# The last FFN's up-projection by seven products of quarters, with the sums' low parts made on VectorE

## The chip, the cores and the metric

One NeuronCore of a Trainium2 chip runs the whole program. The metric is device time in microseconds (us), median over runs. PE is TensorE (matmuls), PEld its weight loads, DVE VectorE, ACT ScalarE, POOL GpSimd, SP the engine that issues the DMAs.

## The reference, cut to what matters

Two layers (width 1024) over 1024 prompt tokens and 8 samples of one token each. Each layer adds a recurrent mixer and then a gated FFN (inner width 2816); a last RMSNorm gives the output.

```python
def swiglu(h, w_up, w_down):
    g, u = jnp.split(h @ w_up, 2, axis=-1)
    return (jax.nn.silu(g) * u) @ w_down
...
        x = x + mix
        x = x + swiglu(rmsnorm(x, norm_ffn[layer]), ffn_w_up[layer], ffn_w_down[layer])
    return (rmsnorm(x, norm_final), ...
```

## The kernel before, in words

Tokens lie on the free axis, in two parts: A (columns 0 to 511) and B (512 prompt columns and the 8 samples, 520 in all). Every dense product is a float32 product made of three single-pass ones: an operand is split into a high part (`wh`, `xh`, `hidh`: the value rounded to fp32r, written by ACT) and a low part (`wl`, `xl`, `hidl`: value minus high part), and PE adds high x high, high x low and low x high in PSUM. Weights come in blocks of 128 x 1024 into a ring of four slots; ACT makes `wh` of each (L1162), POOL `wl` (L1428). A block of an up-projection is eight 128-row slices of the input width for 128 output rows.

The inner width is 22 tiles `f`, taken in 11 pairs `g`. For a pair PE does four `up` units (gate and up of two tiles, `dense`, L807) and then eight `down` units of the pair before (L862). In part B a unit's 520 columns are two matmuls of 260 in two PSUM banks; four banks (0 to 3) go round over the units, and a unit may start only when DVE has emptied its bank. DVE multiplies gate and up by the norm's factor `rsB` and with each other (L1598, L1835), ACT does SiLU, POOL a second multiplication (L1534); DVE makes `hidl` (L1841) and adds each `down` unit to `xB` (L1822). The last pair of B is done in two halves of 260 columns (`down_half`, L878; L2101 adds them), so that the final norm of the first half overlaps the second.

`order()` writes one list of items for the whole program, and every engine walks it in that order; so an instruction of an engine stands behind all items ahead of it there. `("up",1,A,g,q)` is a unit, `("xs",n,m)` the squares of norm `n`, `("mx",1,B,h)` the split of head tile `h` of the mixer's result, `("nrm",n)` and `("nrv",n)` norm `n`'s column sum and root. The program ends with FFN 1 of A, output projection 1 of B (`out`, 8 units) and FFN 1 of B.

Of the kernel before, what the change touches and what calls it, by code (L numbers as in the profile page):

```python
# [9 lines left out]
ALU = mybir.AluOpType  # L10
# [33 lines left out]
def _columns():  # L44
    at = 0
    for name, n in (("gmix0", 8), ("gmix1", 8), ("gffn0", 8), ("gffn1", 8), ("gfin", 8), ("blr", 2),
# [12 lines left out]
         (A, None), (B, "gffn1"), (B, None))  # L59
# [3 lines left out]
N_FFN = {(0, A): 2, (0, B): 4, (1, A): 6, (1, B): 8}  # L63


def order():
# [4 lines left out]
    def ffn(L, X, n_next, at, halves=False):  # L71
        for g in range(NG):
            for q in range(4):
# [21 lines left out]
        if halves:  # L95

            for c in range(2):
                for m in range(KT):
                    add(("dh", c, X, m))
                    if m:  # L100
                        add(("xe", c, m - 1))
                    if c and m == 2:
                        add(("ne", 0))
                    if c and m == 4:
                        add(("nr",))
                    if c and m == 6:
                        add(("nx", 4))
                add(("xe", c, KT - 1))
            add(("nx", 5))
            add(("nx", 6))  # L110
            add(("nx", 7))
            add(("fe", 0))
            add(("ne", 1))
            add(("fe", 1))
            return
        for m in range(KT):
            add(("down", L, X, NG - 1, m))
            if m:
                add(("xs", n_next, m - 1))
        add(("xs", n_next, KT - 1))  # L120
# [120 lines left out]
    def rows(X):  # L241
# [19 lines left out]
class Plan:  # L261


    def __init__(self):
# [3 lines left out]
        used = [None] * 4  # L268
# [7 lines left out]
        for x in it:  # L276
# [3 lines left out]
            if k not in ("sm", "in", "z", "out", "up", "down", "dh", "rg", "s1"):  # L280
# [11 lines left out]
            cur += nb  # L292
# [8 lines left out]
            self.free[u] = before  # L301
            e = "A" if k == "rg" else "D"
# [15 lines left out]
            elif k == "dh":  # L318
                g = NG - 1
                if x[1:] == (0, B, 0):  # L320
                    new = [NB + B_FFN + 4 + g * 6, NB + B_FFN + 5 + g * 6]
                    down["dh"] = [len(self.blocks), len(self.blocks) + 1]
                else:
                    for n in down["dh"]:
                        src_end[n] = u
# [2023 lines left out]
```

## Time and profile before

| | us |
|---|---|
| median of 3 runs | 2490.19 (2488.18 to 2491.6) |
| profiled execution, its own time | 2490.38 |
| its span | 2488.6 |
| PE busy | 2434.4 (98%) |
| DVE / ACT / POOL busy | 1007.4 (40%) / 870.9 (35%) / 1098.4 (44%) |

The span goes from the first to the last instruction of the trace; the execution's own time is 1.8 us longer. Matmuls are pipelined, so a row gives 0.28 us for one of 260 columns whose successor starts earlier; the pace is read from starts. PE's granted clock is in the top tenth in all 40 slices of the page.

### The profile page before, as it was taken

The page shows a single profiled execution, that of the slowest core. Times are in us where ns is not written, and L with a number is a line of the kernel's source. Part 1 is how long each engine was busy: PE and PEld are TensorE (multiplying, and loading weights), DVE is VectorE, ACT ScalarE, POOL GpSimd, SP SyncE. Part 2 cuts the span into 40 slices and gives each one's busy share as a digit, 9 for nine tenths or more (in the row PEclk, how much of TensorE's full clock was granted, in tenths as well). Part 3 has the DMA queues.
Part 4 walks back from the last instruction along what each step waited for, and adds up shares of the span by engine and source line. Part 5 has one row for each costly group of instructions (what it writes and reads, how often), then busy time and mean ns, then how long its engine had stood idle before and what let it go on. Part 6 is the DMA issues. An engine that isn't in the chain of part 4 may idle for free.

```text
span 2488.6 us, 37223 instructions
## 1 busy us (share of the span) xinstructions
PE 2434.4 (98%) x15510; PEld 2194.1 (88%) x15510; DVE 1007.4 (40%) x1712; ACT 870.9 (35%) x1155; POOL 1098.4 (44%) x605
## 2 busy tenths in 40 slices
PE   8999999899999999999999899999999999999998
PEld 6889997688887977999999889988887889999998
DVE  4513255334444435543333443344434443222224
ACT  5431135234223355443333244343432334222223
POOL 2722145555465344544354450043545544544453
PEclk9999999999999999999999999999999999999999
DMA  8863373321324477422222274432232334222222
GB/s 302 307 222 136 136 255 118 105 84 63 123 69 134 161 258 265 152 73 94 85 78 94 77 256 179 168 95 78 81 116 96 119 118 163 93 87 93 94 85 86
DMA packets 102246, 335.88 MB, mean 135 GB/s; under 512 B 12288, under 2 KB 16192, under 8 KB 102080
## 3 DMA queue, kind: packets, MB, share of 16 engines
q1 hardware_dynamic: 102080, 333.52, 39.3%
q8 instruction: 123, 2.02, 0.3%
q14 instruction: 43, 0.35, 0.0%
HBM read 255.20 MB, written 76.16 MB: 133 GB/s over the span
## 4 chain that ended last, share of the span: by engine, by line
PE 88%; DVE 5%; POOL 2%; issue 2%; ACT 1%; DVEq 1%; POOLq 1%; DMA 1%; SPq 0%; ACTq 0%
PE ps L807 63%; PE ps L862 18%; POOL wl L1428 1%; DMA wr<-in_wblk 1%; PE ps L902 1%; PE ps L958 1%; PE ps L956 1%; PE ps L831 0%; DVE mixl L1812 0%; ACT wh L1162 0%; DVE sq L1598 0%; POOLq L1445 0%; PE ps L1019 0%; PE ps L1016 0%; PE ps L962 0%
## 5 line engine op out<-in xcount | busy, mean ns | idle before, releaser
L1428 POOL TENSOR_TENSOR wl<-wr,wh 128x1024 fp32r<-128x1024 f32 (+1 forms) x328 | 791.5, 2427 | 553.2 <-ACT wh L1162 552.9
L807 PE MATMUL ps<-xh,wh 128*128 128x260 f32 (+2 forms) x3296 | 881.8, 322 | 6.6 <-issue 2.6
L807 PE MATMUL ps<-xl,wh 128*128 128x260 f32 (+2 forms) x3296 | 868.8, 318 | 0.0
L807 PE MATMUL ps<-xh,wl 128*128 128x260 f32 (+1 forms) x3280 | 866.8, 319 | 0.0
L807 PEld LDWEIGHTS ps<-xh,wh 128*128 128x128 f32 (+1 forms) x3296 | 543.6, 188 | 60.9 <-issue 17.9
L807 PEld LDWEIGHTS ps<-xl,wh 128*128 128x128 f32 (+1 forms) x3296 | 543.0, 187 | 44.8 <-issue 2.4
L807 PEld LDWEIGHTS ps<-xh,wl 128*128 128x128 f32 x3280 | 541.5, 188 | 44.9
L1162 ACT ACTIVATE wh<-wr 128x1024 fp32r<-128x1024 f32 (+1 forms) x332 | 342.6, 1044 | 291.3 <-DMA wr<-in_wblk 283.8
L862 PE MATMUL ps<-hidh,wh 128*128 128x260 f32 (+1 forms) x1024 | 280.8, 328 | 20.3 <-POOL wl L1428 10.3
L862 PE MATMUL ps<-hidl,wh 128*128 128x260 f32 (+1 forms) x1024 | 277.5, 324 | 0.0
L862 PE MATMUL ps<-hidh,wl 128*128 128x260 f32 (+1 forms) x1024 | 276.6, 324 | 0.0
L1287 ACT ACTIVATE sq<-sq 128x512 f32<-128x512 f32 (+1 forms) x88 | 55.9, 635 | 610.0 <-DVE sq L1598 609.9
L862 PEld LDWEIGHTS ps<-hidh,wh 128*128 128x128 f32 x1024 | 172.2, 190 | 42.5 <-issue 14.0
L1822 DVE TENSOR_TENSOR xB<-ps,xB 128x520 f32<-128x520 f32 x184 | 128.6, 699 | 170.4 <-PE ps L862 106.5
L1534 POOL TENSOR_TENSOR sq<-sq,rsB 128x520 f32<-128x520 f32 x44 | 60.1, 1365 | 293.2 <-ACT sq L1287 293.2
L862 PEld LDWEIGHTS ps<-hidh,wl 128*128 128x128 f32 x1024 | 172.1, 190 | 16.0
L862 PEld LDWEIGHTS ps<-hidl,wh 128*128 128x128 f32 x1024 | 172.6, 191 | 14.4
L1534 POOL TENSOR_TENSOR sq<-sq,rsA 128x512 f32<-128x512 f32 x44 | 57.4, 1305 | 277.7 <-ACT sq L1287 277.5
L1835 DVE TENSOR_TENSOR hf<-ps,sq 128x512 f32<-128x512 f32 (+1 forms) x88 | 61.0, 693 | 292.6 <-PE ps L807 278.8
L1822 DVE TENSOR_TENSOR xA<-ps,xA 128x512 f32<-128x512 f32 x192 | 129.2, 687 | 106.9 <-PE ps L862 78.5
L1292 ACT ACTIVATE hidh<-hf 128x512 fp32r<-128x512 f32 (+1 forms) x88 | 55.9, 635 | 209.7 <-DVE hf L1835 209.7
L1598 DVE TENSOR_TENSOR sq<-ps,rsB 128x520 f32<-128x520 f32 x44 | 30.8, 699 | 186.3 <-PE ps L807 180.2
(373 smaller groups left out, 2314.1 us busy)
## 6 DMA issues: line engine op xcount, KB each, us to landing
wr<-in_wblk SPq DMA_DIRECT2D x328, 512.0 KB, 3.6
split<-wh SPq DMA_DIRECT2D x64, 512.0 KB, 5.3
split<-wl SPq DMA_DIRECT2D x64, 512.0 KB, 6.3
wh<-split SPq DMA_DIRECT2D x64, 512.0 KB, 3.2
wl<-split SPq DMA_DIRECT2D x64, 512.0 KB, 4.2
xr<-in_xT SPq DMA_DIRECT2D x8, 260.0 KB, 6.3
xB<-in_xT SPq DMA_DIRECT2D x8, 260.0 KB, 6.3
out_yT<-xB SPq DMA_DIRECT2D x8, 260.0 KB, 2.2
```

Of the source, the lines that this page charges most:

```text
L807: mm = pe.matmul(ps[0:cols, b + c, 0:n], wt[:, w], xt[:, e:e + n], start=first, stop=end)
L862: mm = pe.matmul(ps[:, b + c, 0:n], wt[:, w], xt[:, t + lo:t + lo + n], start=first, stop=end)
L902: mm = pe.matmul(ps[:, b + c, 0:n], lhsT, src[0:p, lo:lo + n], start=True, stop=True)
L956: pe.matmul(ob, QZ[X][:, h * C:(h + 1) * C], S[:, (h // 2) * P:(h // 2 + 1) * P], start=True, stop=False)
L1162: act.activation(hi, raw, ACT.Copy).then_inc(s_hi, 1)
L1287: act.activation(t, t, ACT.Silu).then_inc(s_si, 1)
L1292: act.activation(hidh[:, t], hf[:, t], ACT.Copy).then_inc(s_hh, 1)
L1428: pool.tensor_tensor(lo, raw, hi.bitcast(F32), ALU.subtract).then_inc(s_lo, 1)
L1534: pool.tensor_tensor(t, t, rs[X][:], ALU.mult).then_inc(s_sr, 1)
L1598: mm = v.tensor_tensor(cut(dst, X), src, cut(rs[X][:], X), ALU.mult)
L1822: v.tensor_tensor(t, bank(pl.bank[u], X), t, ALU.add).then_inc(s_evd, 1)
L1835: v.tensor_tensor(cut(hf[:, t:t + W[X]], X), bank(pl.bank[u], X), cut(sq[q // 2][:, 0:W[X]], X), ALU.mult).then_inc(s_evd, 1)
```

## The change

For each tile `f` of the last FFN (layer 1, part B) the weights are seen as a 2 x 2 matrix of quarters: rows gate and up, columns the two halves of the input width, each quarter four 128 x 128 blocks (512 columns of SBUF). The input is 2 x 2 too: halves of the width, halves of the 520 columns (Q = 260). The four results (gate and up of two column halves) come from seven products of quarters or of sums of quarters instead of eight. The sums of the input are made once, those of the weights (`s1` to `s4`) for each `f`.

- Loads: two blocks of `f` into `wqr[f % 2]` (`weight_set`); the `down` blocks of the last FFN have slots of their own.
- `set_sums` ("wS"): four DVE subtractions or additions of 128 x 512. `set_hi` ("wH"): four ACT copies (1024, 512, 1024, 1024 columns). Low parts: `set_lo`, POOL, three quarters from HBM as 128 x 512 instructions; `sums_lo` ("wL"), DVE, the four sums as two of 128 x 1024. `down_lo` is four of 128 x 512 on POOL for a pair.
- `product` ("sp", f, i): 4 k-steps x 3 matmuls of 260 columns. Products 2 and 4 use banks 4 and 5, the others go round with banks 0 to 3. `products_sum` and `first_product` add the products up: one ACT copy of 260, seven DVE additions of 260, then SiLU of the gate on ACT (520) and a product of gate and up on DVE (520, two inputs in SBUF). POOL's multiplication is gone.
- The input must be normalised before it is split: `scaled` (8 DVE instructions of 520), `quarter_sum` (4 of 1040), `quarter_hi` (7 ACT copies of 1040), `quarter_lo` (7 DVE of 1040).
- For that, `out` of B with its squares now stands after the `up` units of A's pair 9, ahead of the `down` units of A's pair 8; the `mx` items are earlier; the work on the input goes between A's remaining units. A's final norm and output go into B's FFN (f = 4 to 20).

```diff
-    ffn(1, A, 7, merge(rows(B), scan(...), ...
-                       {(8, 4): [("ue", 0), ("dma", "smp1out")], (9, 0): [("ue", 1)], (9, 2): mix(1, B)[0:2],
-                        (9, 3): mix(1, B)[2:4], (9, 4): mix(1, B)[4:6], (10, 0): mix(1, B)[6:8]}))
-    out(1, B, 8, {2: [("nrm", 7), ("nrv", 7)], ...
-    ffn(1, B, 9, {}, halves=True)
+    ffn(1, A, None, merge(rows(B), scan(...), ...
+                          {(8, 2): mix(1, B)[4:6], (8, 4): [("ue", 0), ("dma", "smp1out")], (9, 0): [("ue", 1)] + mix(1, B)[6:8],
+                           (9, 1): mix(1, B)[0:2], (9, 2): mix(1, B)[2:4], (9, "end"): outs,
+                           (9, "down", 2): [("nrm", LAST)], (9, "down", 3): [("nrv", LAST)],
+                           (9, "down", 5): [("wS", 0)], (9, "down", 6): [("xn", 0)], (9, "down", 7): [("xn", 1), ("xn", 2)],
...
+    for f in range(2, NF):
...
+        elif f % 2:
+            places = ((f - 2, "down", 6), (f - 1, 0), (f - 1, 1), (f - 1, 2), (f - 1, 4))
+        else:
+            places = ((f - 1, 3), (f - 1, 4), (f - 1, 5), (f - 1, "down", 1), (f - 1, "down", 4))
+        for n, p in enumerate(places):
+            put(p[0], p[1:], ("wH", f, n - 1) if n else ("wS", f))
+        put(places[4][0], places[4][1:], ("wL", f, 2))
+        last = (2, 1) if f == 2 else (3, 0) if f == 3 else (f - 1, 5) if f % 2 else (f - 1, "down", 6)
+        put(last[0], last[1:], ("wL", f, 3))
...
+                for k in range(KT // 2):
+                    w, e = slice(PIECE[i] * 512 + k * P, PIECE[i] * 512 + (k + 1) * P), slice(k * Q, (k + 1) * Q)
+                    for wt, xt, first, end in ((wqh[f % 2], xqh[i], k == 0, False), (wqh[f % 2], xql[i], False, False),
+                                               (wql[f % 2], xqh[i], False, k == KT // 2 - 1)):
+                        mm = pe.matmul(ps[:, b, 0:Q], wt[:, w], xt[:, e], start=first, stop=end)
...
+            def set_lo(f, j):
+                if j > 1:
+                    return
+                pool.wait_ge(s_qhi, 4 * f + j + 1)
+                pool.wait_ge(s_wsum, f + 1)
+                for n in range(*PAIRS[j]):
+                    e = slice(512 * n, 512 * n + 512)
+                    last = pool.tensor_tensor(wql[f % 2][:, e], wqr[f % 2][:, e], wqh[f % 2][:, e].bitcast(F32), ALU.subtract)
...
+            def set_sums(f):
+                a11, a12, a21, a22, s2, s1, s4, s3 = (wqr[f % 2][:, 512 * n:512 * n + 512] for n in range(8))
+                v.drain()
+                v.wait_ge(s_wq[f % 2], 32 * (f // 2 + 1))
+                v.tensor_tensor(s1, a21, a22, ALU.add)
+                v.tensor_tensor(s3, a11, a21, ALU.subtract)
+                v.drain()
+                v.tensor_tensor(s2, s1, a11, ALU.subtract)
+                v.drain()
+                v.tensor_tensor(s4, a12, s2, ALU.subtract).then_inc(s_wsum, 1)
...
+            def products_sum(it, f, i):
...
+                if i == 1:
+                    v.tensor_tensor(gsum[:, 0:Q], part(1), p1[:], ALU.add).then_inc(s_evd, 1)
+                elif i == 3:
+                    v.tensor_tensor(usum[:], part(3), p1[:], ALU.add).then_inc(s_evd, 1)
+                elif i == 4:
+                    v.tensor_tensor(p1[:], part(4), usum[:], ALU.add)
+                elif i == 5:
+                    v.tensor_tensor(gsum[:, Q:2 * Q], part(5), p1[:], ALU.add).then_inc(s_evd, 1)
+                else:
+                    v.tensor_tensor(usum[:], part(6), usum[:], ALU.add).then_inc(s_evd, 1)
+                    v.drain()
+                    v.tensor_tensor(hf[:, t + Q:t + 2 * Q], part(4), usum[:], ALU.add).then_inc(s_evd, 1)
+                    v.tensor_tensor(hf[:, t:t + Q], usum[:], part(2), ALU.subtract).then_inc(s_evd, 1)
+                    v.drain()
+                    v.wait_ge(s_gsi, f + 1)
+                    v.tensor_tensor(hf[:, t:t + 2 * Q], hf[:, t:t + 2 * Q], gsum[:], ALU.mult).then_inc(s_hm, 1)
```

DVE in a pair of the last FFN, before: four units of gate and up (`L1598`, `L1835`) and eight `down` units into `xB`.

```order
L1598 TENSOR_TENSOR sq_65<-ps,rsB 128x520 [waits unit]
L1835 TENSOR_TENSOR hf<-ps,sq_65 128x520 [waits unit,sr]
L1598 TENSOR_TENSOR sq_66<-ps,rsB 128x520 [waits unit]
L1841 TENSOR_TENSOR hidl<-hf,hidh 128x520 [waits hh]
L1835 TENSOR_TENSOR hf<-ps,sq_66 128x520 [waits unit,sr]
L1822 TENSOR_TENSOR xB<-ps,xB 128x520 [waits unit] x2
L1841 TENSOR_TENSOR hidl<-hf,hidh 128x520 [waits hh]
L1822 TENSOR_TENSOR xB<-ps,xB 128x520 [waits unit] x6
```

The same place in the change, an odd `f` from its product 3 to the first `down` units (`wqr` holds the weights' quarters and sums, `p`, `usum` and `gsum` the sums of products).

```order
L1932 TENSOR_TENSOR usum<-ps,p_116 128x260 [waits unit]
L1903 TENSOR_TENSOR wqr_97<-wqr_97 128x512 [waits wq0]
L1904 TENSOR_TENSOR wqr_97<-wqr_97 128x512
L1906 TENSOR_TENSOR wqr_97<-wqr_97 128x512
L1908 TENSOR_TENSOR wqr_97<-wqr_97 128x512
L1934 TENSOR_TENSOR p_116<-ps,usum 128x260 [waits unit]
L1936 TENSOR_TENSOR gsum<-ps,p_116 128x260 [waits unit]
L1938 TENSOR_TENSOR usum<-ps,usum 128x260 [waits unit]
L1940 TENSOR_TENSOR hf<-ps,usum 128x260
L1941 TENSOR_TENSOR hf<-usum,ps 128x260
L1944 TENSOR_TENSOR hf<-hf,gsum 128x520 [waits gsi]
L2153 TENSOR_TENSOR xB<-ps,xB 128x520 [waits unit] x2
```

Ahead of the first `down` sum there are now four sums of weights, five of products and the product of gate and up. DVE's next rows there, to the end of the `down` units:

```order
L2174 TENSOR_TENSOR hidl<-hf,hidh 128x520 [waits hh]
L2153 TENSOR_TENSOR xB<-ps,xB 128x520 [waits unit] x3
L1916 TENSOR_TENSOR wql_99<-wqr_97,wqh_101 128x1024 [waits qhi]
L2153 TENSOR_TENSOR xB<-ps,xB 128x520 [waits unit] x2
L1916 TENSOR_TENSOR wql_99<-wqr_97,wqh_101 128x1024 [waits qhi]
L1903 TENSOR_TENSOR wqr_98<-wqr_98 128x512 [waits wq1]
L1904 TENSOR_TENSOR wqr_98<-wqr_98 128x512
L1906 TENSOR_TENSOR wqr_98<-wqr_98 128x512
L1908 TENSOR_TENSOR wqr_98<-wqr_98 128x512
L2153 TENSOR_TENSOR xB<-ps,xB 128x520 [waits unit]
```

Two low parts and the sums of the next set now stand between `down` sums. DVE at the end of A's last FFN, before (the 16 `down` units of pairs 9 and 10; two of the 16 are in the row ahead):

```order
L1835 TENSOR_TENSOR hf<-ps,sq_66 128x512 [waits unit,sr]
L1822 TENSOR_TENSOR xA<-ps,xA 128x512 [waits unit] x2
L1841 TENSOR_TENSOR hidl<-hf,hidh 128x512 [waits hh]
L1822 TENSOR_TENSOR xA<-ps,xA 128x512 [waits unit] x14
```

and the first rows of that place in the change (`xq` and `xqr` are quarters of B's input, `xqh` and `xql` their parts):

```order
L2153 TENSOR_TENSOR xA<-ps,xA 128x512 [waits unit] x2
L1896 TENSOR_TENSOR xql_83<-xq,xqh_90 128x1040 [waits xh]
L2174 TENSOR_TENSOR hidl<-hf,hidh 128x512 [waits hh]
L2153 TENSOR_TENSOR xA<-ps,xA 128x512 [waits unit] x2
L1896 TENSOR_TENSOR xql_84<-xq,xqh_91 128x1040 [waits xh]
L2153 TENSOR_TENSOR xA<-ps,xA 128x512 [waits unit] x2
L1896 TENSOR_TENSOR xql_85<-xqr_80,xqh_92 128x1040 [waits xh]
L2153 TENSOR_TENSOR xA<-ps,xA 128x512 [waits unit]
L1916 TENSOR_TENSOR wql_99<-wqr_97,wqh_101 128x1024 [waits qhi]
L2153 TENSOR_TENSOR xA<-ps,xA 128x512 [waits unit]
L1896 TENSOR_TENSOR xql_86<-xqr_81,xqh_93 128x1040 [waits xh]
```

Seven `xql`, two `wql` and four sums of weights now stand between the same 16 sums.

## Rows read from the trace of the kernel before

**Rows 1.** The page: busy time of each engine, and granted clock in 40 slices.
```profile
PE 2434.4 (98%) x15510; PEld 2194.1 (88%) x15510; DVE 1007.4 (40%) x1712; ACT 870.9 (35%) x1155; POOL 1098.4 (44%) x605
...
PEclk9999999999999999999999999999999999999999
```
**Rows 2.** Windows: busy time by engine; output projection of B, then two pairs.
```profile
2046.00:2092.40 46.40, 46.40 (x382) 45.88 (x381) 18.17 (x22) 15.43 (x22) 16.15 (x12) 1.00 0.58 205
...
2300.00:2334.60 34.60, 34.60 (x290) 34.60 (x290) 9.61 (x14) 8.66 (x11) 16.80 (x9) 1.00 0.28 92
2334.60:2369.20 34.60, 34.60 (x290) 34.60 (x290) 9.61 (x14) 8.58 (x11) 16.80 (x9) 1.00 0.28 92
```
**Rows 3.** The chain that ended last: start us, us; one pair of the last FFN.
```profile
2221.00 23.03 PE ps L807 x192
2244.04 11.60 PE ps L862 x96
2255.63 23.07 PE ps L807 x192
```
**Rows 4.** Timeline of PE in `down_half`: start us, us; weights change at each.
```profile
2472.82 0.28 PE L878 MATMUL ps<-hidh,wh 128*128 128x260 f32 x1
2472.94 0.28 PE L878 MATMUL ps<-hidl,wh 128*128 128x260 f32 x1
```
**Rows 5.** Groups, 2060 to 2440 and 2440 to 2489: busy us, mean ns, idle before.
```profile
L1822 DVE TENSOR_TENSOR xB<-ps,xB 128x520 f32<-128x520 f32 x78 | 54.6, 700 | 66.0 <-PE ps L862 46.1 <-PE ps L807 18.6
...
L1534 POOL TENSOR_TENSOR sq<-sq,rsB 128x520 f32<-128x520 f32 x21 | 27.5, 1310 | 147.8 <-ACT sq L1287 147.8
...
L2101 DVE TENSOR_TENSOR xB<-ps,xB 128x260 f32<-128x260 f32 x16 | 6.8, 428 | 6.5 <-PE ps L878 6.4
```
**Rows 6.** `hidl`: count, shortest/median/longest ns, first and last start.
```profile
L1841 DVE TENSOR_TENSOR hidl<-hf,hidh x20: 687/690/1623, 2112.0 to 2420.7; 128x520 fp32r<-128x520 f32 x20
```
**Rows 7.** Timeline of DVE and POOL near 2118 and 1976 us.
```profile
2117.29 2.40 POOL L1428 TENSOR_TENSOR wl<-wr,wh 128x1024 fp32r<-128x1024 f32 x1 [0.79 <-ACT wh L1162]
...
2118.62 1.62 DVE L1841 TENSOR_TENSOR hidl<-hf,hidh 128x520 fp32r<-128x520 f32 x1 [0.70 <-ACT hidh L1292]
...
1974.02 7.12 POOL L1428 TENSOR_TENSOR wl<-wr,wh 128x1024 fp32r<-128x1024 f32 x3
...
1976.58 2.25 DVE L2088 TENSOR_TENSOR oc<-oc,oq 128x32 f32<-128x32 f32 x1
1978.90 2.28 DVE L2090 TENSOR_TENSOR vm<-oc,gt 128x32 f32<-128x32 f32 x1
```
**Rows 8.** Timeline of DVE and POOL where B's mixer result is split.
```profile
1985.73 5.22 POOL L1428 TENSOR_TENSOR wl<-wr,wh 128x1024 fp32r<-128x1024 f32 x2
...
1986.00 5.50 DVE L1812 SCALAR_TENSOR_TENSOR mixl<-vm,par,mixh 128x520 fp32r<-128x520 f32 x2 [2.23 <-ACT mixh L1280]
...
2009.89 8.07 POOL L1428 TENSOR_TENSOR wl<-wr,wh 128x1024 fp32r<-128x1024 f32 x3
...
2011.02 4.66 DVE L1814 TENSOR_TENSOR mixl<-vm,mixh 128x520 fp32r<-128x520 f32 x2 [3.12 <-ACT mixh L1282]
```
**Rows 9.** Who waited for whom, 1660 to 2489 us: total, times, longest.
```profile
PE ps L892 <- POOL rsB L1451: 1.3, 1, 1.3
PE ps L862 <- POOL wl L1428: 1.2, 2, 0.6
PE ps L862 <- DVE xA L1822: 1.2, 1, 1.2
```
**Rows 10.** Groups of ACT: the copies behind `wh` and one of 260 columns.
```profile
L1162 ACT ACTIVATE wh<-wr 128x1024 fp32r<-128x1024 f32 x328 | 341.2, 1052 | 284.4 <-DMA wr<-in_wblk 283.8
...
L1201 ACT ACTIVATE rsB<-ps,par 128x260 f32<-128x260 f32 x1 | 0.5, 478 | 1.1 <-PE ps L886 1.1
```
**Rows 11.** Timeline of PE's `down` unit in A, three matmuls.
```profile
1880.16 0.39 PE L862 MATMUL ps<-hidh,wl 128*128 128x512 f32 x1
1880.39 0.40 PE L862 MATMUL ps<-hidh,wh 128*128 128x512 f32 x1
```

More of the change, by code:

```diff
@@ L84, in ffn @@
                     add(("nrm", N_FFN[L, X]))
+            for s in at.get((g, "end"), ()):
+                add(s)
             if g:
@@ L87, in ffn @@
                     add(("down", L, X, g - 1, m))
+                    for s in at.get((g, "down", m), ()):
+                        add(s)
                     if m == 1:
@@ new lines, in order @@
+    for g in range(NG):
+        first, second = ((3, 0), (3, 2)) if g == 0 else ((2 * g + 2, 5), (2 * g + 3, 0)) if g < NG - 1 else ((NF - 1, 3), (NF - 1, 5))
+        put(first[0], first[1:], ("wD", g, 0))
+        put(second[0], second[1:], ("wD", g, 1))
+    for m in range(KT):
+        put(4 + m + m // 2, (2,), ("xs", 8, m))
+    put(16, (0,), ("nrm", 8), ("nrv", 8))
+    for m in range(0, KT, 2):
+        put(17 + m // 2, (1,), ("fin", m))
+        put(17 + m // 2, (4,), ("fin", m + 1))
+        put(17 + m // 2, (6,), ("fo", m))
@@ L279, in __init__ @@
                 self.rs_end[x[1]] = rs_cur[NORMS[x[1]][0]]
-            if k not in ("sm", "in", "z", "out", "up", "down", "dh", "rg", "s1"):
+            if k not in ("sm", "in", "z", "out", "up", "down", "dh", "rg", "s1", "sp"):
                 continue
@@ L301, in __init__ @@
             self.free[u] = before
+            if k == "sp":
+                i = x[2]
+                if i == 0:
+                    count["A"] += 1
+                    self.ev[u] = ("A", count["A"])
+                else:
+                    self.ev[u] = ("D", count["D"] + (0, 1, 6, 2, 5, 3, 4)[i])
+                    if i == 6:
+                        count["D"] += 6
+                self.evac[x] = self.ev[u][1]
+                continue
             e = "A" if k == "rg" else "D"
@@ L317, in __init__ @@
                 new = [NB * x[1] + B_FFN + (0 if g == 0 else 4 + (g - 1) * 6) + q]
[L318 to L325, printed above, removed]
-                    self.blk[u] = down["dh"]
+            elif k == "dh" or k == "down" and x[1:3] == (1, B):
+                continue
             elif k == "down":
@@ L997, in gla_sample_end @@
                     pe.wait_ge(s_q2, 1)
-                    pe.matmul(ps[:, 5, 64:128], ones, osq[:], start=True, stop=True).then_inc(s_qm2, 1)
+                    pe.matmul(ps[:, 5, 64:128], ones, osq[:], start=True, stop=True).then_inc(s_qm, 1)
             def mlstm_columns(X):
@@ L1101, in _ @@
                     pass
+                elif k == "sp":
+                    product(u, *v)
                 elif k == "dh":
@@ L1604, in x_split @@
                 X, g = NORMS[n]
-                if not g:
+                if not g or n == LAST:
                     return
```

350 lines of the change are left out of this document (285 added, 65 removed), and 5 rows, old and new, of the table outs.

## The prediction

> **What bounds the kernel now.** I read the page's busy times first: PE 2434.4 us of 2488.6, and its granted clock is in the top tenth in every slice, the 2.4 GHz level [rows 1]. Then the windows (their columns: stretch, length, then busy time and count of PE, PEld, DVE, ACT and POOL, clock, DMA share, GB/s): in the output projection of B and in the pairs of the last FFN PE is busy for the whole length, with DVE at 9.61 us and POOL at 16.8 us of 34.6 [rows 2]. A pair takes 34.63 us from start to start, 23.04 for 192 `up` matmuls and 11.6 for 96 `down` matmuls [rows 3], so 0.120 us for a matmul of 260 columns. Nearly all PE idle time behind 1660 us is in three short waits [rows 9]. So a matmul saved here is saved in the end, if nobody else becomes late; and the DVE has 25 us of room in a pair.
>
> **What is removed.** A product has 12 matmuls, a tile `f` 84 where it had 96. Over 22 tiles that is 264 matmuls. In `up` before, two matmuls in a row had the same weights; in a product each has others. `down_half` already works like that, and its starts are 0.12 apart [rows 4]. So the price is 264 x 0.120 = **31.7 us** off. A unit (12 matmuls, also a `down` unit of B) is 1.445 us, a pair of the change 22 units, 31.8 us. "TensorE: Matmul & The Clock Gate" of the Trainium skill, Back-to-back issue gap, gives N/2.4 + 2.5 ns, 111 ns at 260; the rows are 9 ns above it. By the page the saving would be 29.3 us, 2.4 less; the measurement decides.
>
> **What the other engines get.** DVE durations: 0.70 for 520 columns out of PSUM, 0.428 for 260 [rows 5], so 1.05 ns a column; with two inputs in SBUF 0.69 for 520 [rows 6], and by the same slope 0.68 for 512, 1.22 for 1024, 1.24 for 1040 (estimates). A drain costs 0.07: L2090 starts that much after L2088 ends [rows 7]. A pair on DVE: 14 sums of products 6.0, 8 sums of weights 5.5, 4 low parts 4.9, 2 products of gate and up and 2 `hidl` 2.8, 8 `down` sums 5.6, 24 drains 1.7: 26.4 us of 31.8, where it had 9.6. ACT: two sets of copies, 3584 columns each, at 1.05 for 1024, and two `down` blocks, 9.6; two 260-column copies at 0.48 and four of 520 at 0.67, by the slope between these two rows [rows 10], 3.6; 13 us. POOL: L1534 does 520 columns in 1.31 [rows 5], so 10 pieces of 512 are 13 us, less than the 16.8 before. ACT and POOL stay far from the bound. Loads are as many bytes as before.
>
> **Where DVE is late, in a pair.** An odd `f`, t = 0 at the start of its first product. Product 3 is over at 4 x 1.445 = 5.8; its last matmul ends 0.16 behind the next start (a row is 0.28 long, the starts 0.12 apart [rows 4]), so DVE starts at 6.0. Behind it stand `usum` 0.43, the four weight sums with three drains 2.93, five sums of products with four drains 2.43, the product of gate and up with its drain 0.76, and the first `down` sum 0.70: 7.25, to 13.2. PE wants that bank for the third `down` unit at 9 x 1.445 = 13.0. With the way back PE waits 0.3. Further on, a `wL` (1.29) between two `down` sums (0.70 each) makes 2.9 where PE gives 2.89, and `wL`, four sums and `down` 7 make 5.8 from the end of `down` 6, with 5.78 till product 3 wants the bank: some 0.1 each. So 0.5 in a pair if nothing collides.
>
> POOL collides. `hidl` started at 2118.62 while a POOL instruction ran from 2117.29 to 2119.69, and took 1.62 in place of 0.69; it ended 0.55 behind POOL's end. Two instructions of 32 columns took 2.25 and 2.28 under three POOL instructions of 2.4 [rows 7]. Sums out of PSUM are not touched: their mean over 78 is 0.700 [rows 5]. So a DVE instruction with two SBUF inputs waits for the running POOL instruction, and gets in before the next: L1812 twice took 5.50 beside two POOL instructions in 5.22, L1814 twice 4.66 beside three in 8.07, where undisturbed three take 7.12 [rows 7, 8]. "SBUF — State Buffer" of the Trainium skill, SBUF: two separate sides, says that the shared port pair is an exclusive lock for the whole instruction and that the loser fully blocks. By that rule the trace agrees, and it speaks against a change that gives DVE 16 such instructions in a pair in place of two.
>
> The collision on the path is the product of gate and up. Its set's sums end at 9.3; POOL's three low parts then run back to back, 9.4 to 10.7, 12.0 and 13.3. DVE wants the pair at 11.8, waits till 12.0 if all is in time, and 1.3 us more if it comes 0.2 later. So the pair's stall is between 0.5 and 2.2 (0.3 + 1.3 + the small ones with one more collision); I take 1.1, nearer the lower end, since the plan meets the gap. It recurs at the nine odd `f` from 3 to 19 (the last has no set to make): 9 x 1.1 = **10 us**, bounds 4.5 and 20. In an even `f` DVE has 6.9 us of work in 10.1, and its banks are wanted four units later: nothing.
>
> **The passage from A to B.** Behind A's pair 10 stand the 16 `down` units of A, 6 matmuls of 0.23 [rows 11], 22.0 us. DVE has 16 sums of 512, about 0.61 each when queued, 9.8; seven `xl` 9.1; two `wL` 2.6; four sums 2.9; `hidl` 0.7: 25.1. POOL still makes two low parts of 2.4 and three of 1.3, 8.7; half of that as waiting of DVE gives 29.5. Four banks of A leave DVE 3.2 of lag, so PE waits 29.5 - 22.0 - 3.2 = **4.3** (0 if nothing collides, 9 if all does). Ahead of that DVE is less full. `out` of B now starts right behind A's `up` units of pair 9, about 1988, where the last sample head ends at 1981.18 [rows 7]; DVE then has 7.1 us of sums, `hidl` and six or so `mixl`, more with the collisions that stood there [rows 8], so PE waits 2 or 3 at its first k-steps and loses the 1.2 and 0.6 that it lost there [rows 9]: **+1**, bounds -1 and +4. B's loads and its norm lie under 55 us of A. A's final norm adds eight products of 512 and a reciprocal of 512 to DVE in f = 16 to 20, up to 0.7 in an odd `f`: **+1**, bounds 0 and 3. The end (`down_half`, last norm) is the same code, with its weights long there: 0.
>
> **Sum.** 2490.4 (the profiled execution's own time, 0.2 above the median) - 31.7 + 10 + 4.3 + 1 + 1 = **2475**. With the lower bounds 2490.4 - 31.7 + 4.5 - 1 = 2462, with all upper ones 2490.4 - 31.7 + 20 + 9 + 4 + 3 = 2495.
>
> **Rivals.**
> - *DVE keeps up.* The handovers are shorter than I take them, POOL's pieces fall beside DVE's: time 2463, range 2458 to 2467. For it: my stall without collisions is only 0.5 in a pair, and 5 us of DVE's time is free. Against it: two rows of the chain have no margin. Chance 0.2.
> - *DVE becomes the bound, slower.* Every second one of the 16 instructions with two SBUF inputs meets a whole POOL piece of 1.31: 10.5 us, so DVE needs 36.9 for a pair where PE needed 34.6 before: (36.9 - 31.8) x 10 + 6 of passages - 31.7 = +25, 2515. It decides from a stall of (31.7 - 6) / 10 = 2.6 in a pair, that is DVE waiting 8 us in a pair. For it: POOL is busy for 13 of 31.8 us, and all sixteen are queued among it. Against it: `set_lo` waits for the sums, so it never meets those four, and most of `wL` come later. Chance 0.13, with what lies just above 2495.
> - *Given back in full, within 0.2%.* The pair's stall is 2 us (the product of gate and up meets the third piece each time, and `wL` one) and the passage costs 9: 2490.4 - 31.7 + 18 + 9 + 2 = 2488. Chance 0.15.
> - *The passage fails.* ACT waits in order for a ring block ahead of `wH` or `xh`, and product 0 of f = 0 starts some 8 us late; the pairs are as I think: 2483. It is in the forecast's upper range.
>
> **How the numbers follow.** Mine 0.52 (2468 to 2484). Within 0.2% (5 us, about what a measurement of this kernel can tell from no change) 0.15, slower 0.13, faster 0.72. The range leaves out half of the slower case and the lowest end: 2461 to 2490.
>
> **What the changed kernel's profile would show.** Product matmuls 0.120 apart; a pair of 32.9 us with PE idle in front of the third `down` unit, released by DVE's `xB` sum; DVE busy 26 to 29 us in a pair; the product of gate and up 0.9 long or more where undisturbed it is 0.69, sums out of PSUM at 0.43; PE gaps of some 4 us in all in A's last 16 `down` units. A pair above 34.4 would show the second rival, one of 31.9 the first. I would be wrong at the root if product matmuls took longer than 0.120, through weights that change each time beside three writing engines.

## The result, and the profile after

The changed kernel takes 2496.64 us, median of 12 runs (2491.53 to 2500.49), beside 2490.26 of before on the same chip (12 runs, 2486.53 to 2491.79): a ratio of 1.0025, interval 1.0016 to 1.0034. It is slower by a little more than what can be told from no change. The profiled execution took 2495.07 us, 4.7 above the one of before. The page of the changed kernel, span and busy times:

```profile
span 2493.1 us, 37403 instructions
...
PE 2412.8 (97%) x15246; PEld 2165.7 (87%) x15246; DVE 1200.8 (48%) x1987; ACT 910.4 (37%) x1222; POOL 1071.3 (43%) x627
```

The 264 matmuls are gone, and PE is busy 21.6 us less [rows 1]; the rest of the span is waiting. The chain, one ordinary pair (start us, us; L1023 is the product, L1054 a `down` unit):

```profile
2187.88 15.89 PE ps L1023 x132
...
2204.69 1.37 DVE wqr L1903
2206.06 1.70 DVEq L1905
...
2207.84 0.69 DVE wqr L1906
...
2210.41 0.43 DVE usum L1938
...
2211.79 0.73 DVE hf L1944
2212.51 0.62 DVE xB L2153
2213.18 9.00 PE ps L1054 x72
2222.18 7.35 PE ps L1023 x60
```

132 matmuls in 15.89 us are 0.120 each, as forecast, so the saving was made. "TensorE: Matmul & The Clock Gate" of the Trainium skill, Back-to-back issue gap, has a formula for a single matmul by which the gap would be 0.111 (an estimate); the row is above it, as before. The pair takes 34.30 us where it took 34.63 [rows 3]. The windows of four pairs, two ordinary ones and the two in which A's final norm runs (columns as in [rows 2]):

```profile
2187.88:2222.18 34.30, 32.34 (x267) 31.86 (x266) 25.76 (x39) 12.48 (x17) 15.11 (x11) 1.00 0.27 93
2256.14:2291.31 35.17, 32.64 (x266) 31.94 (x266) 26.97 (x39) 13.00 (x18) 16.39 (x12) 1.00 0.26 91
2360.00:2398.60 38.60, 35.59 (x267) 34.56 (x266) 28.50 (x41) 17.02 (x21) 14.63 (x10) 0.91 0.29 96
2398.60:2435.26 36.66, 33.89 (x266) 33.09 (x266) 29.95 (x43) 11.96 (x16) 15.01 (x10) 0.95 0.34 116
```

DVE is not the bound: it has 8 us to spare in a pair in which PE waits. What PE waits for, 2097 to 2470 us (total, times, longest), and in the passage, 2046 to 2097:

```profile
PE ps L1054 <- DVE usum L1938: 12.9, 9, 2.5
PE ps L1054 <- DVE xB L2153: 5.3, 10, 0.7
...
PE ps L1054 <- DVE xA L2153: 4.5, 2, 2.3
PE ps L1054 <- POOL wl L1663: 1.4, 1, 1.4
```

The larger wait is once a pair, and not where the forecast has it: PE stands before the second `down` unit, whose bank is that of product 6, and which `usum` (L1938) reads. Some 0.6 us more go at the third, whose bank the first `down` sum empties. The timelines of DVE, POOL and PE there:

```profile
2204.69 1.37 DVE L1903 TENSOR_TENSOR wqr<-wqr 128x512 f32<-128x512 f32 x1 [0.46 <-issue]
2205.99 1.77 DVE L1904 TENSOR_TENSOR wqr<-wqr 128x512 f32<-128x512 f32 x1
2207.84 0.69 DVE L1906 TENSOR_TENSOR wqr<-wqr 128x512 f32<-128x512 f32 x1
```
```profile
2202.97 2.55 POOL L1691 TENSOR_TENSOR dwl<-dwr,dwh 128x512 fp32r<-128x512 f32 x2 [0.82 <-ACT dwh L1405]
2205.68 1.54 POOL L1674 TENSOR_TENSOR rsA<-rsA,sq 128x512 f32<-128x512 f32 x1 [0.16 <-issue]
2209.44 4.22 POOL L1684 TENSOR_TENSOR wql<-wqr,wqh 128x512 fp32r<-128x512 f32 x3 [2.23 <-DVE wqr L1908]
```
```profile
2210.90 0.51 PE L1054 MATMUL ps<-hidh,dwh 128*128 128x260 f32 x2 [1.38 <-DVE usum L1938]
```

A weight sum takes 0.69 undisturbed. The first started under the second half of `down_lo` (L1691) and ended 0.54 behind POOL's end (2205.52), the second under the addition of A's squares (L1674) and ended 0.54 behind that one's (2207.22): together 1.8 us late. PE pays for them with 1.38 us at the second `down` unit and 0.58 at the third. The product of gate and up (L1944), which the forecast lets collide with `set_lo` (L1684), took 0.73 here. Groups of DVE over nine pairs, 2120 to 2430 us:

```profile
L1916 DVE TENSOR_TENSOR wql<-wqr,wqh 128x1024 fp32r<-128x1024 f32 x36 | 46.9, 1302 | 3.2
L1904 DVE TENSOR_TENSOR wqr<-wqr 128x512 f32<-128x512 f32 x18 | 21.0, 1168 | 0.0
L1903 DVE TENSOR_TENSOR wqr<-wqr 128x512 f32<-128x512 f32 x18 | 17.3, 963 | 3.1 <-issue 1.8
L1944 DVE TENSOR_TENSOR hf<-hf,gsum 128x520 f32<-128x520 f32 x18 | 15.9, 886 | 1.6
L1906 DVE TENSOR_TENSOR wqr<-wqr 128x512 f32<-128x512 f32 x18 | 14.3, 795 | 1.3
```

**The balance.** The first product starts at 2096.48, the first tile's matmul of before at 2092.99: 3.5 later. From there to the first `down_half` unit it is 371.3 us, before 370.2; the 2808 matmuls of that stretch at their pace (11.56 us for 96) would take 338.1, so some 33 us are lost inside. The starts of the even tiles' first products (2153.45, 2187.72, ... 2435.09) split them: six ordinary pairs of 34.36 on average lose 15.4 (2.6 each against 31.8), the two with the norm, 38.8 and 36.7, lose 11.9, the stretch ahead of the pairs 5.0, the last tiles 0.9. The end is as long as before. 3.5 + 1.1 + 0.1 is the 4.7.

### The profile page after: what moved, and what is told of

Its sections match the earlier page's. It is cut to its first block, busy times and chain, and to the rows that moved or that the text cites. A ratio compares the mean times of both kernels' runs of the same rounds, so it can differ in the third digit from the quotient of the medians.

```text
span 2493.1 us, 37403 instructions
## 1 busy us (share of the span) xinstructions
PE 2412.8 (97%) x15246; PEld 2165.7 (87%) x15246; DVE 1200.8 (48%) x1987; ACT 910.4 (37%) x1222; POOL 1071.3 (43%) x627
## 3 DMA queue, kind: packets, MB, share of 16 engines
q1 hardware_dynamic: 102080, 333.52, 38.8%
## 4 chain that ended last, share of the span: by engine, by line
PE 81%; DVE 8%; issue 2%; DVEq 2%; POOL 2%; POOLq 1%; ACT 1%; DMA 1%; SPq 0%; ACTq 0%
PE ps L965 52%; PE ps L1054 17%; PE ps L1023 6%; POOL wl L1663 1%; POOLq L1668 1%; DMA wr<-in_wblk 1%; DVE wql L1916 1%; PE ps L1093 1%; PE ps L1149 1%; PE ps L1147 1%; DVEq L1905 1%; DVE hf L1944 0%; PE ps L989 0%; DVE wqr L1903 0%; DVE sq L1855 0%
## 5 line engine op out<-in xcount | busy, mean ns | idle before, releaser
L1663 POOL TENSOR_TENSOR wl<-wr,wh 128x1024 fp32r<-128x1024 f32 (+1 forms) x262 | 635.6, 2437 | 518.0 <-ACT wh L1355 517.6
L965 PE MATMUL ps<-xh,wh 128*128 128x260 f32 (+3 forms) x2592 | 740.5, 333 | 6.3 <-issue 2.2
L965 PE MATMUL ps<-xl,wh 128*128 128x260 f32 (+3 forms) x2592 | 727.2, 328 | 0.0
L1355 ACT ACTIVATE wh<-wr 128x1024 fp32r<-128x1024 f32 (+2 forms) x266 | 274.2, 1042 | 236.2 <-DMA wr<-in_wblk 227.9
L1054 PE MATMUL ps<-hidh,wh 128*128 128x512 f32 (+1 forms) x704 | 215.5, 347 | 25.3 <-POOL wl L1663 11.0
L1054 PE MATMUL ps<-hidl,wh 128*128 128x512 f32 (+1 forms) x704 | 211.9, 341 | 0.0
L1054 PE MATMUL ps<-hidh,wl 128*128 128x512 f32 (+1 forms) x704 | 211.3, 341 | 0.0
L1023 PE MATMUL ps<-xqh,wqh 128*128 128x260 f32 x616 | 175.4, 285 | 2.5 <-issue 1.7
L1023 PE MATMUL ps<-xqh,wql 128*128 128x260 f32 x616 | 174.1, 283 | 0.0
L1023 PE MATMUL ps<-xql,wqh 128*128 128x260 f32 x616 | 173.6, 282 | 0.0
L1684 POOL TENSOR_TENSOR wql<-wqr,wqh 128x512 fp32r<-128x512 f32 x66 | 91.2, 1411 | 174.1 <-DVE wqr L1908 171.5
L1054 PEld LDWEIGHTS ps<-hidh,wh 128*128 128x128 f32 x704 | 121.9, 190 | 47.3 <-issue 16.1
L1054 PEld LDWEIGHTS ps<-hidh,wl 128*128 128x128 f32 x704 | 121.6, 190 | 15.8
L1054 PEld LDWEIGHTS ps<-hidl,wh 128*128 128x128 f32 x704 | 122.0, 190 | 14.4
```

What stands on the lines that cost most here:

```text
L965: mm = pe.matmul(ps[0:cols, b + c, 0:n], wt[:, w], xt[:, e:e + n], start=first, stop=end)
L1023: mm = pe.matmul(ps[:, b, 0:Q], wt[:, w], xt[:, e], start=first, stop=end)
L1054: mm = pe.matmul(ps[:, b + c, 0:n], wt[:, w], xt[:, t + lo:t + lo + n], start=first, stop=end)
L1355: act.activation(hi, raw, ACT.Copy).then_inc(s_hi, 1)
L1663: pool.tensor_tensor(lo, raw, hi.bitcast(F32), ALU.subtract).then_inc(s_lo, 1)
L1684: last = pool.tensor_tensor(wql[f % 2][:, e], wqr[f % 2][:, e], wqh[f % 2][:, e].bitcast(F32), ALU.subtract)
```

## Experiments

Theory P: POOL's instructions that read SBUF prolong DVE's weight sums, and so make `usum` late; what stands there is `down_lo` and the squares, not `set_lo`. Ratios are to the kernel before on the same chip, and a kernel is named by the number of its experiment.

**1. POOL's work in the last FFN made narrow.** All three kinds work on 8 columns of each piece; PE takes the high parts in place of the low ones, so the FFN's result leaves the low parts of these weights and most of A's squares out.

```diff
                     e = slice(512 * n, 512 * n + 512)
+                    e = slice(512 * n, 512 * n + 8)
...
-                for e in (slice(0, 512), slice(512, 1024)):
+                for e in (slice(0, 8), slice(512, 520)):
```

> The change, but in the last FFN all of POOL's instructions (the low parts of the three quarters, of the down blocks, and A's sums of squares) do 8 columns in place of 512, and PE takes the high part where it took these low parts; all waits stay. Theory P (POOL's instructions make DVE late, by holding up the weight sums in the odd tiles): a pair falls from 34.3 us to 32.4 or less and the two waits of PE in the first down units go; with nine pairs that is 17 to 24 us off 2496, 2472 to 2479. Rival D (DVE's own chain of sums is too long, whatever POOL does): a pair stays at 34 us, 2490 to 2497. Rival C (the clock dips of 3.4 and 6.8 us near the 17th tile are what is lost): pairs as now, and 5 us off at most.

2470.07 us, ratio 0.9931 (0.9917 to 0.9946), 2 us below what was expected. The six ordinary pairs take 32.2 to 32.6 (32.38 on average), the two of the norm 33.6 and 33.4. All weight sums took 0.68 to 0.69 on average. Of the 2.6 us lost in an ordinary pair 2.0 are POOL's doing; 0.6 is left with POOL out of the way.

**2. Only `down_lo` and the squares narrow** (the second part of the diff above and the one below), `set_lo` whole; left out: the low parts of `down` and most of A's squares.

> As before, but only the low parts of the down blocks and A's sums of squares are narrow (8 columns); the three quarters' low parts stay whole on POOL. Theory P, with the collision at the four weight sums: nearly all comes back, 2474 to 2481. My recorded prediction's own place (the product of gate and up waits for the quarters' low parts): nothing changes, 2492 to 2497, since those instructions are still there.

2475.72 us, 0.9955 (0.9939 to 0.9972), ordinary pairs 32.2 to 32.6, 32.41 on average. The product of gate and up still takes 849 ns on average, beside `set_lo`, and in an ordinary pair it costs nothing that can be seen (0.03 us against kernel 1). So the place that the prediction names is not where these pairs lose. In the two pairs of the norm it is one: they take 35.3 and 35.2, 1.7 us more each than in kernel 1. A product of A's final norm (L2430, 1.54 us) stands ahead there, so that the product of gate and up meets POOL's third low part; it ends 0.57 behind it:

```profile
2368.43 1.28 POOL L1686 TENSOR_TENSOR wql<-wqr,wqh 128x512 fp32r<-128x512 f32 x1 [0.66 <-ACT wqh L1401]
2368.63 1.65 DVE L1946 TENSOR_TENSOR hf<-hf,gsum 128x520 f32<-128x520 f32 x1
```

**3. The squares alone narrow**; left out: most of A's squares.

```diff
+                elif n == 8:
+                    pool.tensor_tensor(rs[X][:, 0:8], rs[X][:, 0:8], t[:, 0:8], ALU.add).then_inc(s_acc, 1)
```

> The change with A's sums of squares on POOL 8 columns wide (their result is left out), the down blocks' low parts whole. Theory P: of the some 18 us that narrowing both gave, the squares are the lesser part, since they meet the sums in seven tiles for up to 1.1 us and only those in odd tiles (four of them) count: 2489 to 2495. If the squares were the whole of it: 2475 to 2480.

2490.66 us, 1.0008 (0.9999 to 1.0017), 4 us under the change by the ratios; to kernel 2, with `down_lo` narrow too, it is another 13. An ordinary pair takes 33.28 on average, so there the squares alone give 1.1 us back, and `down_lo` on top of that 0.9. The pairs of the norm stay at 39.2 and 36.7: most of what `down_lo` costs beyond the ordinary pairs is there (5.4 us) and in the stretch ahead of the pairs (2.2).

**4 to 6. The order changed.** `down_lo` at products 3 and 5 of the even tile:

```diff
-        first, second = ((3, 0), (3, 2)) if g == 0 else ((2 * g + 2, 5), (2 * g + 3, 0)) if g < NG - 1 else ((NF - 1, 3), (NF - 1, 5))
+        first, second = ((3, 0), (3, 2)) if g == 0 else ((2 * g + 2, 3), (2 * g + 2, 5)) if g < NG - 1 else ((NF - 1, 3), (NF - 1, 5))
```

> The whole computation. The low parts of the down blocks (and their high parts on ACT) stand at products 3 and 5 of the even tile in place of 5 of the even and 0 of the odd one, so they are over before the odd tile's weight sums. Theory P: the first sum no longer meets a piece; A's sums of squares still do in eight of the tiles; a pair 32.6 to 33.2, 2480 to 2487. Rival D: 2493 to 2498.

The weight sums at product 0 of the odd tile in place of product 3, with `down_lo` left where it was, and then both moves together:

```diff
-            places = ((f - 1, 3), (f - 1, 4), (f - 1, 5), (f - 1, "down", 1), (f - 1, "down", 4))
+            places = ((f - 1, 0), (f - 1, 4), (f - 1, 5), (f - 1, "down", 1), (f - 1, "down", 4))
```

> The whole computation. The four weight sums for an even tile stand at product 0 of the odd tile ahead of it in place of product 3, where DVE has some 3 us free; they will meet POOL's down low parts there, up to 2.6 us, but nothing behind them is due before product 1's bank. Both theories expect a gain, since 2.9 us leave the chain between product 3 and the first down sum: P says that the collision then costs nothing either, a pair 32.2 to 32.6, 2474 to 2480; D says that only the 2.9 us of own work count, of which PE gets 1.4 (its present wait at the second down unit) and the 0.6 behind it: the same number. What tells them apart is the length of the sums: 0.69 each would be against P, 1.3 and more for it.

> The whole computation, both moves at once: the down blocks' low parts at products 3 and 5 of the even tile, the four weight sums at product 0 of the odd tile, where POOL then has nothing of that kind to do. The move of the sums alone gave 2507 (the sums took 1.6 us each there, under POOL's pieces). Theory P (collisions are what costs): the sums take 0.69 each again and a pair falls to 32.3 to 33.0 us: 2476 to 2484. Rival O (sums in one block ahead of the first product's sum are bad by their place, collisions or not): stays above 2500.

They took 2492.9 (1.0023, 1.001 to 1.0036), 2506.88 (1.0078, 1.0063 to 1.0094) and 2511.02 us (1.0083, 1.0064 to 1.0102). All three missed what theory P expected. The third came out as its rival O said, above 2500, but does not tell the place from the collisions: its weight sums still took 0.75 to 1.05 us on average and its product of gate and up 1.49. In the first the sums are nearly clean, but PE now waits in the even tile. Waits of PE, same columns:

```profile
PE ps L1054 <- DVE xB L2153: 7.5, 10, 1.5
PE ps L1023 <- DVE hf L1941: 7.1, 7, 2.2
PE ps L1054 <- DVE usum L1938: 3.9, 3, 1.8
```

With the sums early (the second kernel) they only met `down_lo` as a whole. DVE and POOL of that kernel:

```profile
2206.53 1.60 DVE L1903 TENSOR_TENSOR wqr<-wqr 128x512 f32<-128x512 f32 x1
2208.05 0.68 DVE L1904 TENSOR_TENSOR wqr<-wqr 128x512 f32<-128x512 f32 x1
2208.81 1.63 DVE L1906 TENSOR_TENSOR wqr<-wqr 128x512 f32<-128x512 f32 x1
2210.51 1.62 DVE L1908 TENSOR_TENSOR wqr<-wqr 128x512 f32<-128x512 f32 x1
...
2204.59 2.99 POOL L1691 TENSOR_TENSOR dwl<-dwr,dwh 128x512 fp32r<-128x512 f32 x2 [3.95 <-ACT dwh L1405]
2208.41 3.17 POOL L1691 TENSOR_TENSOR dwl<-dwr,dwh 128x512 fp32r<-128x512 f32 x2 [0.83 <-ACT dwh L1405]
2211.74 1.53 POOL L1674 TENSOR_TENSOR rsA<-rsA,sq 128x512 f32<-128x512 f32 x1 [0.16 <-issue]
```

**7, 8. Sums one by one between `down` units.** For even `f` the four sums go behind four `down` units of the tile before, for odd `f` they are at product 1; the low parts follow later. In the second kernel POOL's last blocks of A are split in halves of 512 columns besides.

```diff
+            places = (None, (f - 1, 4), (f - 1, 5), (f - 1, "down", 6), (f - 1, "down", 6))
+            for n in range(4):
+                put(f - 1, ("down", 2 + n), ("wp", f, n))
...
+                if n > len(pl.blocks) - 9:
+                    pool.tensor_tensor(lo[:, 0:512], raw[:, 0:512], hi[:, 0:512].bitcast(F32), ALU.subtract)
```

> The whole computation. For an even tile the four weight sums stand one by one behind the third to sixth down unit of the odd tile ahead of it, its low parts behind the seventh down unit and at its own product 0; for an odd tile the sums stand at product 1 of the even tile ahead, its low parts at product 5 there and at its own product 0. Between product 3 and the first down sum of an odd tile stand sums of products alone. Theory P: a pair 32.0 to 32.6, 2470 to 2480, faster than both kernels. If DVE's total is what binds (28 us of work and waits in a pair, wherever it stands), it stays at 2488 to 2497.

> The restaged order, and POOL's last eight low parts of the ring's blocks (those of A's last units) as two instructions of 512 columns in place of one of 1024. Theory P for the passage from A to B (there DVE's instructions of 1040 columns took 2.2 to 3.3 us in place of 1.24, under POOL's of 2.4): the waits are shorter but POOL is interrupted more often: 1 to 4 us less than the restaged kernel. If the passage is bound by the order in which ACT and POOL wait for blocks: no change.

2507.62 (1.0067, 1.0049 to 1.0086), where 2470 to 2480 was expected, and 2504.53 us (1.0059, 1.0039 to 1.0078). The two do not differ beyond their intervals, so whether the halves gave the expected 1 to 4 us stays open. PE no longer waits for DVE in the pairs (0.9 us for `usum` in all), but 2.4 us in each for the low parts that come last. POOL's three took 5.72, in the change 4.22. PE of the first kernel there:

```profile
2263.51 0.40 PE L1058 MATMUL ps<-hidh,dwl 128*128 128x260 f32 x2
2266.27 0.36 PE L1027 MATMUL ps<-xqh,wqh 128*128 128x260 f32 x1 [2.37 <-issue]
...
2267.31 0.29 PE L1027 MATMUL ps<-xqh,wql 128*128 128x260 f32 x1
2267.42 0.40 PE L1027 MATMUL ps<-xqh,wqh 128*128 128x260 f32 x1
2267.62 0.42 PE L1027 MATMUL ps<-xql,wqh 128*128 128x260 f32 x1
2267.83 0.42 PE L1027 MATMUL ps<-xqh,wql 128*128 128x260 f32 x1
```

Behind that wait the starts go from 0.12 to 0.21 apart, the 1.2 GHz level, and the run of 168 product matmuls takes 22.04 us. Not every such wait does it. Kernel 7 has nine waits of 2.4 us, and the granted clock fell behind six of them (four runs of 168, 21.9 to 22.1 us); where it held, a run took 20.54. In kernel 8, with nine waits as long, it fell behind four. A fall costs some 1.5 us on top of the wait.

**9, 10. Sums spread over products 2, 2, 3 and 4**, once with `down_lo` early as in 4, once where the change has it.

```diff
+            places = (None, (f - 1, 4), (f - 1, 5), (f - 1, "down", 1), (f - 1, "down", 4))
+            for n in range(4):
+                put(f - 1, ((2, 2, 3, 4)[n],), ("wp", f, n))
```

> The whole computation. The down blocks' low parts at products 3 and 5 of the even tile; the four weight sums for an even tile one by one: two at product 2, one at 3 and one at 4 of the odd tile ahead (in the change all four at product 3), so that no block of them stands in front of a sum of products; low parts and all else as in the change. In the restaged kernel DVE's waits vanished but the sums were ready so late that POOL's low parts held PE 2.4 us in a pair, and the clock fell to its lower level behind each such wait. Theory P (POOL's instructions lengthen the block of sums in front of product 6's sum, on which PE's second down unit waits): that wait goes, 2480 to 2487. If DVE's total load binds: 2493 and more.

> As the kernel with the sums spread, but with the down blocks' low parts where the change has them (product 5 of the even tile and 0 of the odd). Theory P: the second one ends about when the first sums start, so one collision of up to 1.3 us stays, ahead of product 3's sum where DVE has room: within 3 us of its neighbour. If the place of the down low parts matters by itself, 5 us or more apart.

2496.96 (1.0032, 1.0021 to 1.0043) and 2498.47 us (1.0034, 1.0021 to 1.0047). The first missed theory P's 2480 to 2487, the second is within 3 us of it, as expected. The first's product of gate and up took 1275 ns on average, the second's sums 1634 and 1585. Spreading moves the collisions to another instruction.

**11. A's norm moved** to the `down` units of tile 15, its products out of the products of odd tiles:

```diff
-    put(16, (0,), ("nrm", 8), ("nrv", 8))
+    put(15, ("down", 2), ("nrm", 8))
+    put(15, ("down", 3), ("nrv", 8))
...
+        if j % 2:
+            put(j, ("down", 2), ("fin", m))
+            put(j, ("down", 3), ("fin", m + 1))
```

> The change, with A's final norm and its column sum moved from tile 16's first product into tile 15's down units, and the eight products of the final norm out of the products of the odd tiles 17 and 19 into their down units. In the change the pairs of tiles 16 to 19 took 38.6 and 36.7 us, the others 34.3, with DVE waiting 2.9 us for the norm and the clock on its lower level for 10.2 us there. If the norm's place does that (rather than chance of the clock): both pairs 34 to 35, 3 to 7 us less than 2496: 2489 to 2493. If not: 2494 to 2498.

2489.69 us, 0.9999 (0.9989 to 1.0009), 0.26% or 6.5 us under the change by the ratios, as expected. The clock is 1.00 from 2097 to 2450 us, in the change 0.99. The same edit on top of kernel 9:

> The sums spread, the down low parts early, and the norm moved: 2474 to 2483 by theory P, faster than the kernel before by 0.3 to 0.6%. If DVE's load as such binds: no better than 2490.

2495.98 us, 1.0027 (1.0018 to 1.0037), a miss. Among the products of the even tile two `wql` take 1.83 and 1.62 and the product of gate and up 1.62, all under `down_lo`; behind it `hidh` and the next `p` of ACT are late. None of the eight kernels that reorder the pair's sums and low parts gained more than it lost.

**12, 13. `down_lo` taken out of the last FFN, with nothing left out.** A's FFN of the same layer splits the same `down` blocks anyway. Now it stores their parts in `split`, and B's FFN loads both, for pairs 0 to 9. ACT's two copies for each go too.

```diff
+        again = {NB + B_FFN + 8 + 6 * g + i for g in range(NG - 1) for i in range(2)}
...
+                    if g < NG - 1:
+                        sp.dma_start(dwh[i][:].bitcast(F32), a["split"][b + i, 0]).then_inc(s_wd[i], 16)
+                        sp.dma_start(dwl[i][:].bitcast(F32), a["split"][b + i, 1]).then_inc(s_wd[i], 16)
+                        continue
...
-    for g in range(NG):
+    for g in range(NG - 1, NG):
```

> The last FFN's down blocks of groups 0 to 9 are no longer split in it: the FFN before it (A's, the same layer), which splits the same blocks anyway, stores their high and low parts to HBM, and the last FFN loads both parts (1 MB of each block where it loaded 0.5 MB of raw weights). POOL's two low parts and ACT's two copies leave every pair of tiles; everything is still computed. Theory P (what is lost in a pair is POOL's low parts of down and A's squares, which meet DVE's weight sums and other operations with two operands in SBUF): about 1.8 us a pair comes back as in the run that narrowed them, pairs of tiles of about 32.5 us against 34.4 before tile 16, and 2476 to 2483 us in all. Rival T (the transfers take the place: 4 MB more in A's FFN and the doubled load of down in B's hold up the sets' loads or the down units): a wait of PE's down units for the load of down, or units of A's FFN later than before, and 2488 or more. Rival S (the squares and the product alone keep the loss, the down low parts only having stood beside it): pairs of 34 us and 2494 or more.

The second has the norm's move of kernel 11 besides:

> The edit with the stored high and low parts of down, and beside it A's final norm moved to the down units of tile 15 with its products out of the products of odd tiles, as in the run that moved it alone (6.5 us off the change's time). Everything is computed. Theory P with the norm's place a second, independent term: 6 us less than the run with stored parts alone, 2469 to 2477 us, 15 to 20 us under the kernel before. Rival T: 2482 or more. Rival J (the two terms overlap: with down's low parts gone the norm's place costs little, as tiles 16 to 19 waited for both): within 2 us of the run with stored parts alone.

2479.11 us, 0.9966 (0.9953 to 0.9978), and **2473.7 us, 0.9937 (0.9923 to 0.995)**, 16 us under the kernel before by the ratio; both within their expectations, 5.4 us apart. Windows, sums and waits of the second; the second window is the pair into which the norm moved:

```profile
2188.22:2220.78 32.56, 32.10 (x266) 31.77 (x266) 23.95 (x39) 10.58 (x15) 9.67 (x7) 1.00 0.36 130
2318.72:2352.70 33.98, 33.28 (x268) 32.23 (x268) 24.90 (x39) 14.47 (x19) 9.36 (x7) 1.00 0.34 125
2352.70:2384.85 32.15, 32.04 (x266) 31.79 (x266) 25.33 (x41) 11.35 (x15) 8.05 (x6) 1.00 0.41 148
2384.85:2417.09 32.24, 32.15 (x266) 31.87 (x266) 27.85 (x43) 10.07 (x14) 8.96 (x6) 1.00 0.48 164
```
```profile
L1925 DVE TENSOR_TENSOR wqr<-wqr 128x512 f32<-128x512 f32 x19 | 13.2, 693 | 1.4
L1922 DVE TENSOR_TENSOR wqr<-wqr 128x512 f32<-128x512 f32 x19 | 13.2, 693 | 3.2 <-issue 1.8
```
```profile
PE ps L1073 <- DVE xB L2172: 2.2, 5, 0.5
...
PE ps L1038 <- DVE hf L1960: 0.7, 3, 0.3
```

The wait for `usum` is gone and the `xB` one is 2.2 where it was 5.3. The pairs of tiles 16 to 19 are as short as the others; the pair of tiles 14 and 15 takes 0.9 us more than in kernel 12. 31 MB more are moved, and no wait of PE for them appears.

A's squares are whole in these two kernels, and yet no weight sum is longer than 0.69 on average. POOL has no `down_lo` ahead of the squares, ACT without its copies hands them over earlier, and they are over before the sums start (kernel 12; L1686 the squares, L1915 the first sum):

```profile
2199.80 1.63 POOL L1686 TENSOR_TENSOR rsA<-rsA,sq 128x512 f32<-128x512 f32 x1 [7.27 <-ACT sq L1379]
2202.00 0.69 DVE L1915 TENSOR_TENSOR wqr<-wqr 128x512 f32<-128x512 f32 x1 [0.44 <-issue]
```

So the squares' 1.1 us of kernel 3 is no term of its own: without `down_lo` and the copies an ordinary pair takes 32.66 on average, 1.7 less than in the change, though the squares are still there.

## Why the prediction was wrong

The forecast was 2475 us, range 2461 to 2490; the kernel took 2496.64.

- **What bounds it, and the -31.7.** Right: PE was the bound, the matmuls are 0.120 apart, and kernel 13 has 16 of the 31.7 us in the end.
- **"I take 1.1 ... 9 x 1.1 = 10 us": the step that failed.** It was 2.6 in an ordinary pair. "The collision on the path is the product of gate and up" is wrong in place for these pairs: with `set_lo` whole and the other two narrow (kernel 2) they take 32.4 on average, so the part that was worked out costs 0.6 where 1.1 was taken, and all of that is there without `set_lo` too (kernel 1): it is the working's 0.5 without collisions. Only in the two pairs of the norm does that collision cost 1.7 us each. The list of POOL's work had only the `set_lo` pieces in the odd tile's second half. `down_lo` stands at product 5 of the even tile and product 0 of the odd one, waits for ACT's copies, and runs 1.3 us into the sums' place (2205.52 against 2204.23, the end of `usum` L1932); the squares come right behind. POOL's time was counted at 13 us in a pair without the squares, and was 15.1 to 16.2. The half sentence in the second rival, "`set_lo` waits for the sums, so it never meets those four", is true, and hid that two others can. With the sums 1.8 us longer, `usum` is late at the second `down` unit, a handover that the working goes past: it counted the first `down` sum, for the third. The page "SBUF — State Buffer" of the Trainium skill, SBUF: two separate sides, had been applied to one POOL instruction out of three kinds; the trace agrees with it on all three (weight sums end 0.54 behind `down_lo` and the squares, the product of gate and up 0.57 behind `set_lo`).
- **"A's final norm ... +1".** 6.5 by kernel 11, and 5.4 beside stored parts. The norm's and `fin`'s work puts DVE later still in two odd tiles (waits of 2.3 to 2.5 us), and behind them the clock fell: 0.91 of 38.6 us and 0.95 of 36.7 are 3.5 and 1.8 us, most of the term. No term of the sum allowed for the clock.
- **The passage, +4.3 and +1.** About right: 5.9 us of waits there, and the first product is 3.5 later. A rival mechanism in it, POOL's low parts under DVE's quarter sums, showed itself: 128x1040 took 2.2 to 3.3 where 1.24 was estimated.
- **The rivals.** "Given back in full", 2488, was nearest by size (2 us a pair) and its mechanism was the wrong collision. "DVE becomes the bound" had the right threshold (2.6 in a pair is where the gain is gone) with the wrong picture: DVE is busy 25.8 of 34.3 us, so it is not the bound but late in one place of a pair. Its price of 2.6 stood so near the forecast's own upper bound of 2.2 that 0.13 for the slower side was too little.
- **What the other kernels say of the rest.** The stretch ahead of 2153 loses 5.0 us in the change, 2.8 with `down_lo` narrow (kernel 2) and 1.2 with `set_lo` narrow too (kernel 1). With the squares narrow ACT's copies cost nothing: kernel 2 keeps them, and its stretch ahead, ordinary pairs and pairs of the norm take 54.8, 32.41 and 35.3 us, beside 54.8, 32.66 and 35.3 in kernel 12.
- **Open.** What the remaining 0.6 us of an ordinary pair and 1.2 of the stretch ahead consist of was not taken apart, nor how much of kernel 12's gain comes from the squares being handed over earlier for want of ACT's copies. Whether a block of sums ahead of the first product's sum costs by its place alone (the rival of kernel 6) is open. Why the clock fell behind some waits of 2.4 us and not behind others of the same length is open too.

## What to carry to other kernels

Before an instruction with two SBUF inputs is put on DVE's critical stretch, list every POOL instruction that can run there, by the row of what releases it, not only those that belong to the same data. In a steady loop as full as this one reordering only chose the victim: eight reorderings gained nothing, and taking 5 us of POOL's work out of a pair, by storing what another stage had computed, gave some 15 us (0.9966 against 1.0025). What one instruction of a queue costs depends on those ahead of it: the squares met the sums from behind `down_lo`, and missed them once it and ACT's copies were gone. And a new wait of PE of more than 2 us can cost more than its length: the clock fell behind 10 of 18 waits of 2.4 us in kernels 7 and 8, some 1.5 us each.

## What the runs showed of the hardware

- A DVE instruction with two SBUF inputs that starts under a POOL one ends some 0.55 us behind that one's end (0.54 in the change, 1.37 and 1.77 in place of 0.69; 0.57 in kernel 2; 0.55 in [rows 7]), and gets in ahead of the POOL instruction queued next.
- POOL pays as well: three 128x512 low parts took 4.22 us, but 5.72 in kernel 7, where two of DVE's low parts of 1024 columns stood beside them; the mean over 54 was 1.63 us there, 1.37 in the change.
- TensorE's granted clock fell to the lower level behind single waits of 2.3 to 2.5 us, in stretches where PE was otherwise fully busy, but not behind all of them: behind both in the pairs of the change, behind six of nine in kernel 7, four of nine in kernel 8. Behind the change's waits of 1.4 and 1.7 us in its ordinary pairs (in front of 2314.36 and 2280.03) it held.
